# Cached pages in 25 rotating slots: nine pages of the next sample loaded ahead and begun in the last steps of the current one

## What is computed

```
past = cache[pages].reshape(-1, CACHE_ROW)
rows = concatenate([past, rows_i])
lat_i, kr_i = rows[:, :256], rows[:, 256:]
kn_i = rmsnorm(einsum('...c,chd->...hd', lat_i, w_uk)) * g
s = (q_nope . kn_i + q_rope . kr_i) * scale        # 8 heads
ctx = softmax(s) @ lat_i ;  out = ctx @ w_uv
```

## Time and profile before

| | us |
|---|---|
| runs, median of 3 | 3434.42 (3432.81 to 3442.86) |
| profiled execution, its own time | 3437.44 |
| span of its profile | 3435.7 |
| PE busy | 2760.1 |
| VectorE busy | 2273.9 |
| ScalarE busy | 1043.7 |
| GpSimd busy | 1228.3 |
| bytes moved | 1264.74 MB |

### The profile page before, as it was taken

One profiled execution on the slowest core, in us unless ns is written; L12 is line 12 of the kernel. 1 busy time (PEld: TensorE's weight loads), 2 busy tenths in 40 slices (PEclk: granted clock), 3 DMA queues, 4 the chain that ended last, 5 costly groups with the idle time before them and its releaser, 6 DMA issues.

```text
span 3435.7 us, 39604 instructions
## 1 busy us (share of the span) xinstructions
PE 2760.1 (80%) x11303; PEld 1233.2 (36%) x11303; DVE 2273.9 (66%) x6378; ACT 1043.7 (30%) x4438; POOL 1228.3 (36%) x1077
## 2 busy tenths in 40 slices
PE   7888889969889868979988779889876775666765
PEld 2345554424434323434443244344321231112321
DVE  2454568887787876767776676777766545565455
ACT  1222324424344322433434314434311111111111
POOL 0000014433333434434444434443434443443443
PEclk8989999989989989989989989999987777677777
DMA  8751069999899999999999999999999999999998
GB/s 322 282 185 35 14 237 408 401 385 391 359 394 405 413 378 400 416 383 402 413 407 405 408 387 411 414 410 413 396 414 402 422 421 408 420 389 378 421 420 352
DMA packets 201396, 1264.74 MB, mean 368 GB/s; under 512 B 23689, under 2 KB 44730, under 8 KB 61393
## 3 DMA queue, kind: packets, MB, share of 16 engines
q0 software_dynamic: 150784, 1091.03, 77.8%
q1 hardware_dynamic: 50393, 171.18, 13.0%
HBM read 1258.79 MB, written 3.79 MB: 367 GB/s over the span
## 4 chain that ended last, share of the span: by engine, by line
PE 42%; DMA 29%; DVE 12%; issue 7%; another core or an unknown queue 3%; ACT 3%; POOL 2%; SPq 1%; DVEq 0%; POOLq 0%; ACTq 0%; PEldq 0%
PE bank L1154 15%; DMA ring<-in_uv,work 11%; PE bank L888 7%; DMA mod_mix<-in_uv,work 7%; DMA big<-in_uv,work 6%; PE bank L1004 5%; DVE ring L2036 2%; PE bank L834 2%; PE bank L702 2%; ACT work L1483 1%; DMA ring<-in_w_ada 1%; DMA work<-in_cache_mla 1%; POOL ring L1522 1%; PE bank L640 1%
## 5 line engine op out<-in xcount | busy, mean ns | idle before, releaser
L1154 PE MATMUL bank<-ring,work 128*64 128x512 f32 (+1 forms) x2080 | 903.2, 706 | 242.3 <-ACT work L1483 241.1
L1522 POOL DMA_INDIRECT ring<-in_uv,work x520 | 612.8, 1179 | 900.7 <-PE bank L1154 774.5
L2036 DVE CUSTOM_DVE_ANT_0 ring<-ring,mod_smp 128x1024 f32<-128x1024 f32 x512 | 622.4, 1224 | 261.8 <-DMA ring<-in_uv,work 253.1
L1522 POOL DMA_INDIRECT big<-in_uv,work x260 | 309.8, 1191 | 679.6 <-PE bank L1154 379.3
L1471 ACT ACTIVATE work<-work 128x2 f32<-128x2 f32 x520 | 105.3, 202 | 1457.4 <-DVE work L2036 1440.8
L888 PE MATMUL bank<-big 128*128 128x512 f32 x1024 | 517.9, 629 | 0.0
L1154 PE MATMUL bank<-big,work 128*64 128x512 f32 (+1 forms) x1040 | 324.3, 743 | 155.8 <-ACT work L1483 154.1
L1154 PEld LDWEIGHTS bank<-ring,work 128*64 128x64 f32 (+1 forms) x2080 | 208.8, 152 | 589.0 <-ACT work L1483 349.4
L2036 DVE CUSTOM_DVE_ANT_0 big<-big,mod_smp 128x1024 f32<-128x1024 f32 x256 | 309.8, 1224 | 142.4 <-DMA big<-in_uv,work 138.2
L1154 PE MATMUL bank<-work 128*64 128x512 f32 (+1 forms) x520 | 295.6, 697 | 95.9 <-ACT work L1483 95.7
L1483 ACT ACTIVATE work<-small,work 128x64 f32<-128x64 f32 (+1 forms) x1040 | 303.3, 339 | 145.1 <-DVE work L2046 135.7
(11 more groups left out here) (301 smaller groups left out, 3395.4 us busy)
## 6 DMA issues: line engine op xcount, KB each, us to landing
big<-in_wk SPq DMA_DIRECT2D x48, 1152.0 KB
ring<-in_w_ada SPq DMA_DIRECT2D x64, 768.0 KB
work<-in_cache_mla SPq DMA_DIRECT2D x104, 160.0 KB
ring<-in_uv,work POOLq DMA_INDIRECT x520
big<-in_uv,work POOLq DMA_INDIRECT x260
ring<-in_w_mla_out SPq DMA_DIRECT2D x1, 4096.0 KB, 14.0
big<-in_w_mla_out SPq DMA_DIRECT2D x4, 1024.0 KB, 12.5
mod_smp<-in_cache_mla SPq DMA_DIRECT2D x24, 160.0 KB
```

The costliest lines, as they stand in the source:

```text
L1154: last = mm(out, diag[:, t % 2, j, 0:min(m, HALF)], s[:, D + half * 512:D + (half + 1) * 512], start=(k == 0 and (n < S0 or j == 0)), stop ...
L1522: pool.indirect_dma_start(slot[g % SLOTS], None, T["uv"].rearrange("l e d -> (l e) d"), bass.IndirectOffsetOnAxis(index[:, k * GRP + j:k * ...
L2036: dve.tensor_tensor_reduce(u, u, hb, 1.0, 0.0, ALU.mult, ALU.add, dots[:, at:at + 1]).then_inc(sem("dots_set"), 1)
```

## The change

The pages of all samples rotate through 25 places: the 16 of before and nine new ones in a buffer `pages_ahead` (12,288 bytes in each partition). The bytes for it come from the scratch of the software-generated DMA descriptors, `dynamic_dma_scratch_size`, which goes from its default of 16,384 bytes to 4,096. Pages 0 to 8 of the next sample are loaded in turn `tail - 8` of the current one, pages 9 to 15 in `tail + 5`, behind the context. The first page of the next sample is now projected from turn `tail + 2` on, beside the last steps; where its columns of bank 6 are still read, it waits for the step that reads them. The plan then gives tails at turns 34, 77, 111, 160, 197, 231, 280 and 314 (worked out from lines 333 to 343 with the new step), and the output projection of the samples stays at turn 360.

```diff
-        PGRP = 4
+        PGRP, EARLY = 4, 9
+        pages_ahead = sb("pages_ahead", [P, 3 * D])
-        cached = [cached_all[:, g * ROW:(g + 1) * ROW] for g in range(13)]
-        cached += [mod_smp[:, 2, g * ROW:(g + 1) * ROW] for g in range(3)]
+        page_slots = [cached_all[:, g * ROW:(g + 1) * ROW] for g in range(13)]
+        page_slots += [mod_smp[:, 2, g * ROW:(g + 1) * ROW] for g in range(3)]
+        page_slots += [pages_ahead[:, g * ROW:(g + 1) * ROW] for g in range(EARLY)]
+        cached = lambda r, g: page_slots[(r * NPG + g) % len(page_slots)]
             tail[r_] = t_
-            t_ += 7
+            t_ += 2
@@ SP @@
-                    if t == tail[r - 1] + 4:
+                    if t == tail[r - 1] - 8:
+                        if r >= 2:
+                            sp.wait_ge(sem("ctx_ps"), r - 1)
+                        sp.wait_ge(sem("page_ps"), (r - 1) * NPG + EARLY)
+                        load_pages(r, 0, EARLY)
+                    if t == tail[r - 1] + 5:
                         sp.wait_ge(sem("ctx_ps"), r)
-                        load_pages(r)
+                        load_pages(r, EARLY, NPG)
@@ PE, project_page @@
-                if g == 0 and r:
-                    pe.wait_ge(sem("ctx_ready"), r)
+                if r:
+                    gone = page_at[r, g] - tail[r - 1]
+                    if gone >= 7:
+                        pe.wait_ge(sem("ctx_ready"), r)
+                    elif gone >= 5:
+                        pe.wait_ge(sem("ctx_norm"), r)
+                    elif gone >= 3:
+                        pe.wait_ge(sem("s_shift"), r)
+                    else:
+                        pe.wait_ge(sem("max_diag"), r)
@@ PE, spread_max and DVE, top: the maxima go to columns 256 to 384 of bank 6 @@
-                pe.transpose(pb[6][0:NH, 0:P], tiny[:, 8:8 + NH], ident)
+                pe.transpose(pb[6][0:NH, 2 * P:3 * P], tiny[:, 8:8 + NH], ident)
@@ the program @@
-    nc = bacc.Bacc("TRN2", target_bir_lowering=False, num_devices=1)
+    nc = bacc.Bacc("TRN2", target_bir_lowering=False, num_devices=1, dynamic_dma_scratch_size=4096)
```

More of the change, by code:

```diff
@@ L492, in _, with load_pages @@
             sp.wait_ge(sem("first_set"), 1)
-            def load_pages(r):
-                for g in range(NPG):
+            def load_pages(r, first, end):
+                for g in range(first, end):
                     page = sp.value_load(pages[0:1, r * NPG + g:r * NPG + g + 1], min_val=0, max_val=T["cache_mla"].shape[1] - 1)
-                    ld(cached[g], T["cache_mla"][0, bass.ds(page, 1)].rearrange("a p n -> (a p) n"), f"page_in{g // PGRP}")
-                ld(cached_own[0:1, :], O["rows_s"][0, r:r + 1, 0, 0:KL], f"page_in{NPG // PGRP}")
+                    ld(cached(r, g), T["cache_mla"][0, bass.ds(page, 1)].rearrange("a p n -> (a p) n"), f"page_in{g // PGRP}")
+                if end == NPG:
+                    ld(cached_own[0:1, :], O["rows_s"][0, r:r + 1, 0, 0:KL], f"page_in{NPG // PGRP}")
             def pooling_weights():
@@ L546, in turn @@
                     w.next("table_in", 16)
-                    load_pages(0)
+                    load_pages(0, 0, NPG)
                     ld(O["pst_s"][0, :, 0:STATE - 1, :], T["state_pool"][0, :, 1:STATE, :], "state_out")
@@ L865, in turn_page @@
                 for c in range(KLC):
-                    pe.transpose(pb[7][:, c * P:(c + 1) * P], cached[g][:, c * P:(c + 1) * P], ident)
-                pe.transpose(pb[7][0:ROPE, 2 * P:3 * P], cached[g][:, KL:ROW], ident).then_inc(sem("page_ps"), 1)
+                    pe.transpose(pb[7][:, c * P:(c + 1) * P], cached(r, g)[:, c * P:(c + 1) * P], ident)
+                pe.transpose(pb[7][0:ROPE, 2 * P:3 * P], cached(r, g)[:, KL:ROW], ident).then_inc(sem("page_ps"), 1)
             def project_page(r, g):
@@ L893, in spread_max @@
                 pe.wait_ge(sem("s_max"), r + 1)
-                pe.transpose(pb[6][0:NH, 0:P], tiny[:, 8:8 + NH], ident).then_inc(sem("max_ps"), 1)
+                pe.transpose(pb[6][0:NH, 2 * P:3 * P], tiny[:, 8:8 + NH], ident).then_inc(sem("max_ps"), 1)
             def spread_max2(r):
@@ L905, in context @@
                     at, m = g % 4 * 32, 32 if g < 4 else NH
-                    last = mm(pb[6][at:at + m, 160:160 + KL], ps_all[:, g * NH:g * NH + m], cached[g][:, 0:KL] if g < NPG else cached_own,
+                    last = mm(pb[6][at:at + m, 160:160 + KL], ps_all[:, g * NH:g * NH + m], cached(r, g)[:, 0:KL] if g < NPG else cached_own,
                               start=(g < 4), stop=(g > NPG - 4), skip_group_check=True)
@@ L1884, in top @@
                 dve.wait_ge(sem("max_ps"), r + 1)
-                dve.tensor_reduce(tiny[0:NH, 34:35], pb[6][0:NH, 0:P], AX_X, ALU.max).then_inc(sem("smp_tail"), 1)
+                dve.tensor_reduce(tiny[0:NH, 34:35], pb[6][0:NH, 2 * P:3 * P], AX_X, ALU.max).then_inc(sem("smp_tail"), 1)
                 dve.wait_ge(sem("smp_tail"), r * 2 + 1)
```

## The result

The changed kernel takes 3457.43 us in the median of four runs (3453.40 to 3459.62), the kernel before 3433.61 us on the same chip (3430.82 to 3442.86). The ratio is 1.0061, 95% interval 1.0048 to 1.0074: 21 us slower by the ratio (24 between the medians). I had said 3428 and a range up to 3449, so the time lies outside it. The profiled execution took 3459.62 us (span 3457.8).

The account below looks back on a forecast made before the run. The prediction took the transfers to bind nearly everywhere. Its terms, -7 for page waits, 0 for page work in the tails, +1 for queries and 0 for the scratch, summed to -6 us: 3428 us from a median of 3434.42, range 3407 to 3449.

Parts of the forecast that it names:

- What bounds the kernel: Nearly everywhere the transfers, 4.98 us a turn; only 20.5 us of idle DMA time in the tails could be won.
- Part 1, the page waits: In four tails PE's 29.6 us of waits for cache loads go; taken as 7 us won, bounds 0 and 29.6.
- All of the 29.6 us: Rival for the tails: all of PE's wait for cache loads counts, giving 3405 us; chance 0.05.
- Part 2, page work in the tails: 20 pages, 100 us of PE, move into seven tails and fit PE's idle time; taken as 0, bounds -12 and +39.
- My bound of +39 us: Upper bound for page work in the tails: every 2.8 us delay of `spread_max2` and context comes through, twice in seven tails.
- my own case: The forecast of 3428 us for the whole kernel, with its own range 3419 to 3440; chance 0.47.
- The clock: In the tails filled gaps may keep PE's clock up, freeing up to 41 us; over 0.9 was a sign of right.
- Part 3, the queries: On page turns, 44 query turns instead of 42, one burst more; taken as +1 us, bounds 0 and +3.5.
- Part 4, the scratch: For the gathers, a quarter of the descriptor scratch still suffices, an estimated 28 gathers; taken as 0, at most 77 us.
- the chain of the tail gets longer: Rival in the tails: page work ahead of `spread_max2` and `context` delays DVE, then PE; +12.5 us, 3447; chance 0.18.
- Signs: Right: tail share 1.00, clock over 0.9, DVE's 90% unchanged. Wrong: shares under 0.97, DVE waiting for `spread_max2`, dearer page turns.

Follow-up runs that it names:

- the gap of two: The changed kernel as it is: next sample's first page at the earliest two turns after a sample's last; 1.0061 and 1.0049 of the kernel before.
- the gap of seven: Changed kernel with seven turns, as before, between a sample's last page and the next one's first; early loads and small scratch stay; 0.9971 and 0.9980 of the kernel before.
- the table: Both plans with full work, short queries, short key projections or both; packing costs 24 to 31, 17, 13 and 7 us.
- shortening the queries: Both plans with one of eight parts of the query work from the second pair of tiles on: 1.0005 packed, 0.9955 with seven turns between samples.
- avoiding them: Changed kernel with no page in the query turns of all but the first query group: 3428.71 us, 0.9996 of the kernel before.
- Taking most of these waits away: Changed kernel, PE running the last steps ahead of the pages' large projections: 1.0066; with ACT's squares of the page keys a turn later too: 1.0065.
- both works short: Both plans with one of eight query parts (second to fourth pair of tiles) and one of two key projection parts: 0.9967 packed, 0.9946 with seven turns between samples.
- the overlap with the last steps alone: Changed kernel pausing five turns after the second page of each sample but the first, two pages still beside the last steps: 3429.91 us, 0.9996 of before.

## Why the prediction was wrong, step by step

- **What bounds the kernel: right on the mean, wrong in its use.** Transfers bind (behind the pages the share is 1.01 in both kernels). I took from this that only the idle time already there, 20.5 us, was at stake. That gave a ceiling to the gain and none to the loss.
- **Part 1, the page waits, -7: right.** Alone it measured 0.9971 and 0.9980, 10 and 7 us; the idle time of its tails fell by 6 us. All of the 29.6 us, a rival of mine, did not come.
- **Part 2, page work in the tails, priced 0: the step that failed.** It costs 24 to 31 us (the gap of two against the gap of seven with the same loads). Two sentences carried the error. "The windows show PE with 12 to 24 us idle a tail" took the room for spare; it was time in which PE caught up. And "the page turns that become free lie at the end ... they are worth nothing by themselves" was true at the end and overlooked the beginning. As an estimate from the earlier trace rows, a turn with the expert matmuls alone costs PE 1.87 us of 4.98 at full clock, so PE makes up 3.1 us in it, against 0.6 in a page turn (in a tail it is less, since the last steps and a low clock take their part). The last tail moved from turn 345 to 314, so 31 such turns went from between the pages to where nobody needs them. That the cost hangs on PE's amount of work is shown by the table; that it comes about by catching up in free turns fits all the plans tried, and no trace follows it turn by turn. My bound of +39 us held the size, but for another mechanism, and I had given its half to a rival and not to my own case.
- **The clock: half right.** I wanted over 0.9 in the tails; of the eight rows three show it. A page can meet the low clock: here in the second tail PE's line 905 takes twice its time, at a granted clock of 0.50 (1.2 GHz) from 958.3 to 962.1, and ACT and DVE wait behind it:

```profile
958.34 3.78 PE L905 MATMUL bank<-big 128*128 128x512 f32 x4
...
962.16 0.26 ACT L1356 ACTIVATE bank<-bank 128x128 f32<-128x128 f32 x1 [4.60 <-PE bank L905]
...
962.63 0.30 DVE L1910 TENSOR_TENSOR big<-big,bank 128x136 f32<-128x136 f32 x1 [2.90 <-PE bank L915]
```

  Its projection takes 3.78 us where I had counted 1.91, so the work moved into a tail can be dearer there. The Trainium skill, TensorE: Matmul & The Clock Gate, section Loop structure matters more than you think, has matmuls without gaps stay at the higher clock and those behind a long wait run at the lower. The trace agrees: the tails rose to 0.83 to 0.96 from 0.76 to 0.86. That the higher clock would pay in time was my own step, and the kernel became slower.
- **Part 3, the queries, +1: mis-sized, by the same error.** I counted one burst more (44 against 42) and priced it alone. Behind the bursts that were there already the transfers stood idle longer (5 to 7 us more than before in sum). That the slots stood emptier when they came is my reading; the occupancy of the slots was not measured. How much of the 24 to 31 us is the bursts' can't be split off cleanly: shortening the queries took away 7 to 14 us, and avoiding them 18 to 22, but with more free turns as well.
- **Part 4, the scratch, 0: right**, 1.0001 [0.9986, 1.0016]. The estimate from the Trainium skill, DMA: Bandwidth & Descriptors, section The descriptor swizzle, was that 28 gathers fit in 4096 bytes; no run shows the 28, but eight in flight are not held back.
- **The rival "the chain of the tail gets longer"** named 3447 and was the nearest, but for a reason that fell. DVE did wait for `spread_max2` (14.2 us against 0.2), hardly for the context (0.2 us), and for PE's last step less than before (16.4 against 32.0). Taking most of these waits away changed nothing (1.0066 and 1.0065).
- **Signs.** Of those named as wrong, tails under 0.97 appeared in six of eight, and DVE's wait for `spread_max2` appeared; no page stretch turned dearer at full share: 1500:1548 moves 420 GB/s in 1.01. Of those named as right, the share over the fourth tail and behind it is 0.97 and 0.73, not 1.00, and DVE's 90% did not hold (40.23 of 46.6 us in the first tail, 86% against 93%).

What stays open: some 7 us between the two plans with both works short (7 wide either way), and the 6 to 9 us of the overlap with the last steps alone. Both may be one thing, and neither is far from nothing.

The best version here is the changed kernel with the gap of seven: early loads, pages as before. It measured 0.9971 [0.9957, 0.9986] and 0.9980 [0.9968, 0.9991] against the kernel before, and is 24 to 31 us faster than the changed one.

## What to carry to other kernels

In a loop bound by transfers an engine that is about 10% faster than they are is not off the path: here it was covered only as long as it had turns in which to make up what bursts cost. Before moving its work into a gap, write down how far behind it is when it gets there, how much it gains back per turn of each kind, and how many slots hide the difference; average shares show little of this. The share in the turns behind bursts shows more, if it is summed over all of them and compared over two traces of each kernel; a pair picked out shows nothing, since the kernel before has bad ones too. And part a change that moves loads and work together: here one half won 7 to 10 us and the other lost 24 to 31.

## What the hardware showed that I had not expected

The gathers' packets took longer in the kernel whose transfers paused more: 2683 and 2681 us in two traces against 2673 before, 2667 and 2669 with the gap of seven, and 2663 and 2666 with PE's work short, for the same 150784 packets and 1091.03 MB. So a pause seems to cost its own length and something again. From 500 us on, all packets of the trace take 2896.5 us of an engine before, 2904.2 in the changed kernel and 2886.3 with the gap of seven, in 2935.7, 2957.8 and 2919.1 us. What is left is 39.2, 53.6 and 32.8 us (packets overlap a little, full being 1.01, so only the differences count). So of the 22 us between the spans before and after some 14 are pauses and 8 to 10 longer packets.

Cut into stretches of 3 us from 600 to 2600 us, the traces show where the long packets are. In stretches with a share over 0.99 behind another such stretch a packet of 8192 bytes takes 314 ns in the mean before and 315 in the changed kernel and with the gap of seven, so nothing became dearer there. In stretches under 0.9 it takes 385, 373 and 395 ns, and in a full stretch right behind one under 0.9 329, 346 and 330 (7 to 14 stretches each). Long packets and pauses stand together; which of the two brings the other is not shown, and no run took it apart.
